# Feed-forward products in quads: 448-column matmuls, a stationary token block, and the extra columns added by DVE

## What is computed

```python
D_MODEL = 1024; D_FF = 11 * D_MODEL // 4      # 2816
def swiglu(x, w_in, w_out):
    gate, up = jnp.split(x @ w_in, 2, axis=-1)
    return (jax.nn.silu(gate) * up) @ w_out
def half_ffn(x, g, w_in, w_out):
    return x + FFN_RES * swiglu(rms_norm(x, g), w_in, w_out)
...
for i in range(DEPTH):                        # 2 layers
    yp = half_ffn(yp, ffn_norm1[i], ffn_w_in1[i], ffn_w_out1[i])
    ...                                       # mixer of layer i, then yp += its output
    yp = half_ffn(yp, ffn_norm2[i], ffn_w_in2[i], ffn_w_out2[i])
```

## Time and profile before

| | |
|---|---|
| median of 3 runs | 1105.52 us |
| profiled execution: its time | 1104.89 us |
| profiled execution: its span | 1103.0 us |
| PE busy (matmul) | 1086.1 us, 98% |
| DVE busy | 692.7 us, 63% |
| ACT busy | 520.9 us, 47% |
| POOL busy | 124.7 us, 11% |
| DMA | 172.43 MB, mean 156 GB/s |

### The profile page before, as it was taken

The page is one execution under the profiler, slowest core; times in us unless marked ns, Lnnn a source line. Parts: engine busy times, 40 slices in busy tenths (PEclk is TensorE's granted clock), DMA queues, the critical chain, the costliest instruction groups (busy, mean ns, idle before and its releaser), DMA issues.

```text
span 1103.0 us, 21261 instructions
## 1 busy us (share of the span) xinstructions
PE 1086.1 (98%) x8086; PEld 1068.1 (97%) x8086; DVE 692.7 (63%) x1071; ACT 520.9 (47%) x812; POOL 124.7 (11%) x158
## 2 busy tenths in 40 slices
PE   8999999999999999999999999999999999999997
PEld 7999999998999999999999999999988899999997
DVE  6766665465656766665547666645599776666441
ACT  6544443345665544443335444433466554444332
POOL 5000001100004300000110000011232500000011
PEclk9999999999999999999999999999999999999999
DMA  6544454324333644554434444544332244444531
GB/s 229 193 178 162 152 210 158 133 110 181 130 125 125 203 172 159 179 185 160 164 143 153 166 176 152 202 156 151 132 124 90 109 160 158 180 156 181 179 136 43
DMA packets 24435, 172.43 MB, mean 156 GB/s; under 512 B 3236, under 2 KB 3400, under 8 KB 5832
## 3 DMA queue, kind: packets, MB, share of 16 engines
q1 hardware_dynamic: 22368, 167.45, 42.7%
q0 software_dynamic: 1248, 2.92, 0.7%
q10 hardware_dynamic: 776, 1.48, 0.4%
HBM read 169.28 MB, written 2.57 MB: 156 GB/s over the span
## 4 chain that ended last, share of the span: by engine, by line
PE 92%; DVE 4%; DMA 2%; ACT 2%; issue 1%; SPq 0%; POOL 0%; DVEq 0%; ACTq 0%
PE acc L402 30%; PE acc L404 29%; PE acc L403 29%; DMA raw<-in_w 2%; DVE wlo L389 1%; PE mb L662 0%; ACT whi L365 0%; PE mb L681 0%; DVE rstd L1036 0%; PE mb L588 0%; PE acc L709 0%; ACT work L949 0%; PE mb L423 0%; PE num L597 0%; DVE work L1258 0%
## 5 line engine op out<-in xcount | busy, mean ns | idle before, releaser
L402 PE MATMUL acc<-xhi,whi 128*128 128x288 f32 x1696 | 507.0, 299 | 3.9 <-DVE wlo L389 2.0
L403 PE MATMUL acc<-xlo,whi 128*128 128x288 f32 x1696 | 501.1, 295 | 0.0
L365 ACT ACTIVATE whi<-raw 128x1024 fp32r<-128x1024 f32 (+1 forms) x290 | 326.7, 1128 | 366.5 <-PE acc L404 338.2
L404 PE MATMUL acc<-xhi,wlo 128*128 128x288 f32 x1696 | 499.5, 295 | 0.0
L389 DVE TENSOR_TENSOR wlo<-raw,whi 128x1024 fp32r<-128x1024 f32 (+1 forms) x290 | 386.2, 1332 | 167.9 <-ACT whi L365 157.1
L402 PEld LDWEIGHTS acc<-xhi,whi 128*128 128x128 f32 x1696 | 318.5, 188 | 6.6 <-DVE wlo L389 2.2
L404 PEld LDWEIGHTS acc<-xhi,wlo 128*128 128x128 f32 x1696 | 320.2, 189 | 0.0
L403 PEld LDWEIGHTS acc<-xlo,whi 128*128 128x128 f32 x1696 | 319.3, 188 | 0.5
L402 PE MATMUL acc<-ahi,whi 128*128 128x288 f32 x832 | 247.2, 297 | 0.9 <-DVE alo L1270 0.7
L403 PE MATMUL acc<-alo,whi 128*128 128x288 f32 x832 | 245.4, 295 | 0.0
L404 PE MATMUL acc<-ahi,wlo 128*128 128x288 f32 x832 | 244.6, 294 | 0.0
(11 more groups left out here) (227 smaller groups left out, 606.9 us busy)
## 6 DMA issues: line engine op xcount, KB each, us to landing
raw<-in_w SPq DMA_DIRECT2D x113, 1024.0 KB, 4.8
raw<-in_w SPq DMA_DIRECT2D x32, 1408.0 KB, 5.9
x<-in_xT SPq DMA_DIRECT2D x4, 288.0 KB, 6.8
raw<-in_w SPq DMA_DIRECT2D x4, 256.0 KB, 6.0
work<-row_bounce ACTq DMA_DIRECT2D x1, 640.0 KB, 4.3
work<-in_cst POOLq DMA_DIRECT2D x1, 560.0 KB, 4.2
work<-in_c POOLq DMA_DIRECT2D x1, 514.0 KB, 4.3
out_cp<-work POOLq DMA_DIRECT2D x4, 128.5 KB, 3.9
```

Of the source, the lines that this page charges most:

```text
L365: act.activation(dst, src, ACT.Copy).then_inc(hi_done, 1)
L402: pe.matmul(out, wh, hi[:, k, :], start=(first and n == 0), stop=False)
L403: pe.matmul(out, wh, lo[:, k, :], start=False, stop=False)
L404: mm = pe.matmul(out, wl, hi[:, k, :], start=False, stop=(last and n == len(tiles) - 1))
```

## The change

The feed-forward stages are done in quads of four pieces. xhi and xlo lie side by side in one tensor xs (chunk, hi or lo, token), and ahi and alo in fs. For one weight tile of each of four pieces the kernel now issues:

- one matmul of 512 columns (`edge_products`): the low part of the last 128 tokens is the stationary operand, and the four whi tiles move. All tiles of a quad add up in PSUM bank mb[0] (in ffn_out: all 22 tiles of three quads);
- per piece one matmul of 448 columns (`wide_products`): whi is stationary, and the 288 high columns and the first 160 low columns move. The result takes 448 columns of the bank;
- per piece one matmul of 288 columns: wlo is stationary, and the high columns move.

ACT copies the edge bank to SBUF (`edge_copy`, 512 columns). PE turns each of its four 128 x 128 blocks into columns 160 to 287 of a piece's bank, adding (`edge_turn`). DVE brings out columns 288 to 447 (160 of them, `NEAR`) into `part`, then the 288, and adds the two in SBUF. In ffn_out it adds both to x. whi gets eight slots of 8 tiles, and wlo four. The ffn_out pieces are cut into 8, 7 and 7 tiles (K_CUTS) instead of 11 and 11. `split_hi` now waits for the piece eight before, and `split_lo` for the piece four before. The mixers' pieces keep their three products.

```diff
@@ -35,18 +35,21 @@
 BIG, TINY = 1e30, 1e-30
 Y_VECTOR, Y_SCALAR = ((0, 0), (1, 0), (2, 0)), ((0, 1), (1, 1), (2, 1))
 WARM_UP = 18
-RAW = 2 * (KF // 2)
+SLOT = 8
+RAW = 2 * SLOT
...
 TOK = [(0, 128), (128, 128), (256, 32)]
 
 
-STAGES = [("ffn_in", 22, 44, 8), ("ffn_out", 8, 8, 11), ("mlstm_in", 12, 24, 8), ("mix_out", 4, 8, 8),
-          ("ffn_in", 22, 44, 8), ("ffn_out", 8, 8, 11), ("ffn_in", 22, 44, 8), ("ffn_out", 8, 8, 11),
-          ("swa_in", 6, 24, 8), ("mix_out", 4, 8, 8), ("ffn_in", 22, 44, 8), ("ffn_out", 8, 8, 11)]
+STAGES = [("ffn_in", 22, 44, 8), ("ffn_out", 12, 8, 0), ("mlstm_in", 12, 24, 8), ("mix_out", 4, 8, 8),
+          ("ffn_in", 22, 44, 8), ("ffn_out", 12, 8, 0), ("ffn_in", 22, 44, 8), ("ffn_out", 12, 8, 0),
+          ("swa_in", 6, 24, 8), ("mix_out", 4, 8, 8), ("ffn_in", 22, 44, 8), ("ffn_out", 12, 8, 0)]
...
 
 
         raw = sb("raw", [P, 2, RAW * P])
-        whi = sb("whi", [P, 4, KF // 2, P], F32R)
-        wlo = sb("wlo", [P, 4, KF // 2, P], F32R)
+        whi = sb("whi", [P, 8, SLOT, P], F32R)
+        wlo = sb("wlo", [P, 4, SLOT, P], F32R)
         x = sb("x", [P, KD, T])
-        xhi = sb("xhi", [P, KD, T], F32R)
-        xlo = sb("xlo", [P, KD, T], F32R)
-        ahi = sb("ahi", [P, KF, T], F32R)
-        alo = sb("alo", [P, KF, T], F32R)
+        xs = sb("xs", [P, KD, 2, T], F32R)
+        fs = sb("fs", [P, KF, 2, T], F32R)
...
-                act.wait_ge(piece_done, 4 * it + c - 3)
+            act.wait_ge(landed[(c // 2) % 2], 32 * it + 16 * (c // 4 + 1) - (16 if (c // 2) % 2 == 0 else 0))
+            if c >= 8:
+                act.wait_ge(piece_done, 8 * it + c - 7)
             src = raw[:, (c // 2) % 2, (c % 2) * L * P:(c % 2 + 1) * L * P]
-            dst = whi[:, c % 4, 0:L, :].rearrange("p a b -> p (a b)")
+            dst = whi[:, c % 8, 0:L, :].rearrange("p a b -> p (a b)")
             act.activation(dst, src, ACT.Copy).then_inc(hi_done, 1)
 
         def head_split_hi(act, n):
...
 
         def split_lo(dve, it, c, L):
-            dve.wait_ge(hi_done, 4 * it + c + 1)
+
+            dve.wait_ge(hi_done, 8 * it + c + 1)
+            if c >= 4:
+                dve.wait_ge(piece_done, 8 * it + c - 3)
             src = raw[:, (c // 2) % 2, (c % 2) * L * P:(c % 2 + 1) * L * P]
-            hi = whi[:, c % 4, 0:L, :].rearrange("p a b -> p (a b)").bitcast(F32)
...
                 if before:
                     before(k)
-                wh, wl = whi[:, slot, t, :], wlo[:, slot, t, :]
+                wh, wl = whi[:, c % 8, t, :], wlo[:, c % 4, t, :]
                 pe.matmul(out, wh, hi[:, k, :], start=(first and n == 0), stop=False)
                 pe.matmul(out, wh, lo[:, k, :], start=False, stop=False)
                 mm = pe.matmul(out, wl, hi[:, k, :], start=False, stop=(last and n == len(tiles) - 1))
             return mm
+
+        def wide_products(pe, out, c, tiles, v, first, before=None):
+
+            for n, (t, k) in enumerate(tiles):
+                if before:
+                    before(k)
+                pe.matmul(out[:, 0:T + NEAR], whi[:, c % 8, t, :], near_of(v, k), start=(first and n == 0), stop=False, skip_group_check=True)
+                mm = pe.matmul(out[:, 0:T], wlo[:, c % 4, t, :], v[:, k, 0, :], start=False, stop=False, skip_group_check=True)
+            return mm
+
+        def edge_products(pe, c, tiles, v, first, last, before=None):
+
+            for n, (t, k) in enumerate(tiles):
+                if before:
+                    before(k)
+                mm = pe.matmul(mb[0], v[:, k, 1, NEAR:T], whi[:, c % 8:c % 8 + 4, t, :], start=(first and n == 0),
+                               stop=(last and n == len(tiles) - 1))
+            return mm
+
+        def edge_turn(pe, out, j):
+
+            return pe.matmul(out[:, NEAR:T], edge[:, j * P:(j + 1) * P], ident, start=False, stop=True,
+                             is_transpose=True, skip_group_check=True)
+
...
@@ -473,46 +527,70 @@
                             pe.wait_ge(head_lo, q + 1)
                         if k == KD // 2:
                             pe.wait_ge(lo_done, q + 1)
-                        mm = products(pe, group_bank(q), q, [(k, k), (k + 1, k + 1)], xhi, xlo,
-                                      k == 0, k == KD - 2, before=x_ready if q == 0 else None)
-                        if k == KD - 2:
-                            mm.then_inc(piece_done, 1)
+                        wide_products(pe, wide_bank(q), q, [(k, k), (k + 1, k + 1)], xs, k == 0, x_ready if q == 0 else None)
+
+            n_edge = [0]
+
+            def in_quad(i, it, quad, begun=False):
+
+                c, G = 2 * FIRST_UNIT[i] + 4 * quad, FIRST_GROUP[i] + 4 * quad
+                tiles = [(k, k) for k in range(KD)]
+                pe.wait_ge(hi_done, 8 * it + c + 4)
+                edge_products(pe, c, tiles, xs, True, True).then_inc(edge_mm, 1)
+                for j in range(4):
+                    if not (begun and j < 2):
+                        pe.wait_ge(lo_done, 8 * it + c + j + 1)
+                        if G + j >= 4:
+                            pe.wait_ge(evac, 8 * it + G + j - 3)
+                        wide_products(pe, wide_bank(j), c + j, tiles, xs, True)
+                    if begun and j == 2 and i == 0:
+                        ss_sum()
+                        norm_no[0] += 1
+                    if begun and j < 2:
+                        continue
+                    if j == 2 or not begun and j == 0:
+                        pe.wait_ge(edge_in, 2 * it + n_edge[0] + quad + 1)
+                    for t in (0, 1, 2) if begun and j == 2 else (j,):
+                        edge_turn(pe, wide_bank(t), t).then_inc(piece_done, 1)
...
+            def edge_copy(n):
+
+                act.wait_ge(edge_mm, n)
+                act.activation(edge[:, :], mb[0], ACT.Copy).then_inc(edge_in, 1)
...
+                def quad_work(it, quad):
+
+                    c, G = 2 * FIRST_UNIT[i] + 4 * quad, FIRST_GROUP[i] + 4 * quad
+                    if quad == 0 and i:
+                        split_hi(act, it, c + 4, SLOT)
+                        rms(norm + 1)
+                    edge_copy(2 * it + n_edge[0] + quad + 1)
+                    if quad == 0 and i == 0:
+                        split_hi(act, it, c + 4, SLOT)
+                        rms(norm + 1)
+                    def silu(u):
+
+                        act.wait_ge(gate_ready, 4 * it + f0 + 2 * quad + u + 1)
+                        act.activation(f_silu[:, u, :], f_gate[:, u, :], ACT.Silu).then_inc(silu_done, 1)
+
+                    def prod_hi(u):
+
+                        act.wait_ge(prod_done, 4 * it + f0 + 2 * quad + u + 1)
+                        k = bass.ds(4 * it + 2 * quad + u, 1)
+                        act.activation(ahi[:, k, :], f_prod[:, u:u + 1, :], ACT.Copy).then_inc(ahi_done, 1)
+
+                    if quad:
+                        split_hi(act, it, c + 4, SLOT)
+                    split_hi(act, it, c + 5, SLOT)
+                    silu(0)
+                    split_hi(act, it, c + 6, SLOT)
+                    prod_hi(0)
+                    split_hi(act, it, c + 7, SLOT)
+                    silu(1)
+                    prod_hi(1)
+
+                quad_work(0, 0)
+                with act.Fori(0, KF // 4 - 1) as it:
+                    for quad in (1, 2):
+                        quad_work(it, quad)
+                for quad in (KF // 2 - 2, KF // 2 - 1):
+                    quad_work(0, quad)
...
+                        dve.wait_ge(sum_done, n)
+                        dve.wait_ge(evac, 8 * it + G + j + 1)
+                        dve.tensor_tensor(dst[:, 0:NEAR], dst[:, 0:NEAR], part[:, j % 2, :], ALU.add).then_inc(ready, 1)
+
+                    for u in range(2):
+                        n = 4 * it + f0 + 2 * quad + u + 1
+                        evacuate(2 * u, f_gate[:, u, :], gate_ready)
+                        split_lo(dve, it, c + 4 + 2 * u, SLOT)
+                        evacuate(2 * u + 1, f_up[:, u, :], up_ready)
+                        dve.wait_ge(silu_done, n)
+                        dve.wait_ge(up_ready, n)
+                        dve.wait_ge(evac, 8 * it + G + 2 * u + 2)
+                        dve.tensor_tensor(f_prod[:, u, :], f_silu[:, u, :], f_up[:, u, :], ALU.mult).then_inc(prod_done, 1)
+                        split_lo(dve, it, c + 5 + 2 * u, SLOT)
+                        dve.wait_ge(ahi_done, n)
+                        k = bass.ds(4 * it + 2 * quad + u, 1)
+                        dve.tensor_tensor(alo[:, k, :], f_prod[:, u:u + 1, :], ahi[:, k, :].bitcast(F32), ALU.subtract).then_inc(alo_done, 1)
+
+                quad_work(0, 0)
+                with dve.Fori(0, KF // 4 - 1) as it:
+                    for quad in (1, 2):
+                        quad_work(it, quad)
+                for quad in (KF // 2 - 2, KF // 2 - 1):
+                    quad_work(0, quad)
+
+            def ffn_out(i, norm):
+
```

(18 more changed lines are left out.)

225 lines of the change are left out of this document (109 added, 116 removed).

## The result

The changed kernel takes 1135.45 us (median of 4 runs, 1134.16 to 1136.98), the kernel before 1104.97 in the same comparison: a ratio of 1.028, 95% interval 1.0266 to 1.0294. It is slower by 30.5 us where I forecast 16, and it lies 1.5 us outside my range. Its profiled execution has a span of 1133.6 us; the earlier trace rows belongs to one of 1103.0.

The account below looks back on a forecast made before the run. PE was taken to bound the kernel. 1104.9 us profiled, plus 2.3 (PE's work), 8.2 (waits in three ffn_in) and 5.3 (first ffn_in), gave 1120.7; with 0.6 for the median, 1121 us, range 1091 to 1134.

Parts of the forecast that it names:

- The PE balance: On PE, 528 sets save 20.6 us and 208 turns cost 22.9 us: +2.3 us in all.
- I take the fixed surplus: Each fp32r matmul on PE carries 0.013 us extra whatever its width, so 448 columns take 0.200 us; chance 0.47.
- The rivals of price: Alternative costs of a wide PE matmul: 448 columns at 0.189 us (chance 0.33) or 0.207 us (chance 0.13).
- The covered case: Wide matmuls on PE start 0.189 us apart at 448 columns and 0.215 at 512; chance 0.33.
- The proportional case: Wide matmuls on PE start 0.207 us apart at 448 columns and 0.236 at 512; chance 0.13.
- Waits at the starts: After each ffn_in's first quad PE waits for ACT's fourth whi: 2.5 us in three stages, about 5 in the first.
- the late edge: In each ffn_in's second quad, the edge copy comes after PE wants it, costing another 0.25 us.
- The clock: An idle PE may lose its clock, costing 1.5 us; it may happen once, left in the range.
- Steady loops: In running quads DVE's 10.2 us fit PE's 12.9, and everything is hidden with 1 to 2 us to spare.
- Other places: Last x chunk after ffn_out: nothing, at most 0.7 us in one stage; mixers' splits: nothing, at most 1 us gained.
- The range: Whole kernel 1091 to 1134 us, allowing a lost clock and up to 10 us of thin covers.

Follow-up runs that it names:

- the widths: Changed kernel with the wide matmul at another width, 288 to 512 columns, in each feed-forward stage; single execution 1100.85 us, not comparable.
- The early whi splits: Changed kernel, but in each ffn_in's first quad ACT splits the next quad's third and fourth weight pieces before waiting for the first gate; 1136.94 us.
- filling the waits: Changed kernel, but PE issues 288-column matmuls into an unread bank where it would wait after each ffn_in's first quad; 1129.82 us.
- the wide matmuls in a row: Changed kernel, but each piece issues its eight 448-column matmuls one after the other, then its eight 288-column ones; 1131.25 us.
- all orders that helped: Changed kernel with whi splits and edge copy earlier on ACT, 448-column matmuls in a row, and first two pieces' turns after half the third; 1122.43 us.

## Why the prediction was wrong in size

Point by point, by its own steps:

- *The PE balance.* Failed in size: +2.3 forecast, +10.7 measured (11.1 in ffn_in, -0.4 in ffn_out). The step that failed is "I take the fixed surplus", 0.200 us for 448 columns. No run shows its term, 0.013 us with each fp32r matmul, at 448 columns: the matmul takes 0.204, by the estimate above 17.5 ns over its columns, and 2112 of them at 0.0045 are 9.5 us. The edge matmul was right, 0.227 in the running part against 0.226, and the turns nearly: 0.104 against 0.11. The nearest row was of 288 columns only, and the widths show that one price doesn't carry over: between 288 and 512 columns the surplus lies anywhere from 11 to 19 ns. A cost that is the same for every matmul does not fit these widths, and what its cause is no run tests.
- *The rivals of price.* The covered case, 0.189 for 448 columns and 0.215 for 512, has next to no surplus. It came from two f32 records of 258 columns, which start 0.43 us before the next group. That they could stand for wide fp32r matmuls held a third of my chances, and it was false: no fp32r width here came under 10 ns. The proportional case, in which a matmul's whole time grows with its columns (0.207 for 448), was 2.5 ns too high at 448, and it names 0.236 where 512 columns of the edge take 0.227. The truth lay between the fixed and the proportional one, where I had put no case.
- *Waits at the starts.* Right in place, cause and size: without the late edge 12.5 forecast, 13.0 measured, released by ACT's whi as told. The early whi splits showed that this queue is what PE stood for. The late edge of the second quad is there too, 0.3 us against 0.25, but only where the clock did not fall; a like loss before the third quad I had not seen.
- *The clock.* Failed: "It may happen once, and I leave it in the range", at 1.5 us. It happened at three of the four starts, 4.7 us, and filling the waits made the ffn_in stages 3.9 us shorter. I had leaned on the 2.3 us wait near 245, which left the clock at 1.00. Behind the three waits of 2.66 us the clock fell twice and stayed up once. And the row that I leaned on is not what that wait always brings: in 7 of the 13 changed kernels (this one and its variants) the clock fell right behind the very same wait, now 2.37 us long, as with the wide matmuls in a row, where it ended at 256.15:

```profile
253.50:256.20 2.70, 0.62 (x6) 1.00 0.01 3
257.00:260.40 3.40, 3.40 (x16) 0.50 0.56 148
```

One row of one execution was too little to set the case at once in four.
- *Steady loops.* Right: quads 13.05 apart with PE never idle, DVE 78%, and no change when DVE lost its additions. Thin as the covers are, they held.
- *Other places.* x for the second ffn_in is 0.8 us late, the upper end of what I allowed (0.7); I had costed it at nothing. It stands behind a mix_out, while my working was of the end of an ffn_out; behind the ffn_out stages x was not late, and why it is here no run shows. The mLSTM stage and its mix_out took 1.1 us more, with a longer wait and a fall of the clock that they did not have before.
- *The range.* With the balance as measured, the clock's falls, x, mLSTM, 0.2 more of waits and late edge, and 0.6 given back elsewhere, the sum is 1121 + 8.4 + 4.7 + 0.8 + 1.1 + 0.2 - 0.6 = 1135.6. The upper end of 1134 had room for a lost clock or for a dearer wide matmul, not for both at once.

## What to carry to other kernels

Merging matmuls that share weights saved only the surplus per instruction here, by my estimate 13 ns of 133, and every helper instruction that the merging needs (a turn, 0.104 us) had to be paid out of it: 528 sets saved 15.5 us, with the wide ones in a row, and 208 turns took 21. Before such a change, measure the price of the new width on the chip, since the row of another width was off by a third of the surplus here, 4.5 ns of 13. And where work is done in larger batches, cost the first batch of each stage by itself: the queue that was hidden in the loop stood open there, and moving one instruction only moved the wait to the next in the queue.

## What the runs showed of the hardware that I had not expected

- The next matmul starts 11 to 19 ns after an fp32r matmul's columns' time (0.417 ns a column, my estimate from 0.833 at a granted clock of 0.50), and not evenly: 480 columns have less over (14 ns) than 448 (17) and 416 (19). Within a stream of one width the spacing is not constant either: 448-column ones in a row go anywhere from 199 to 207 ns, while 288-column ones in the kernel before go 132 to 134 throughout.
- A 128-column fp32r matmul against the identity costs the stream the same 0.11 us as an f32 transpose of 128 columns, although the next matmul is recorded 0.06 instead of 0.03 us after it.
- The clock's fall costs more than its wait suggests: 2.66 us of idle PE brought, twice in three, another 1.5 us of loss at a granted clock of 0.50, and 2.3 us of matmuls that nobody reads removed it. The length of the wait alone does not tell whether it happens: before the second and third quads of ffn_in waits of up to 1.97 us left the clock up each time, but of four waits of 2.07 to 2.09 us two were followed by a fall and two were not, and in the second mix_out it fell behind a pause of 1.0 us (with all orders that helped, at 875). Since it falls in one execution and not in another at the same place, a difference of 1.5 us between two traces can be the clock's and not the edit's.
